# Gate products of the second branch in Strassen's form, paired in PSUM banks, copied by ScalarE and added by GpSimd

## The reference

```python
def merge_branches(gates, o_mla, o_conv, o_diff, w_o_mla, w_o_conv, w_o_diff, w_out):
    g = jax.nn.sigmoid(gates).reshape(*gates.shape[:-1], N_BRANCH, D_MODEL)
    y = (g[..., 0, :] * (o_mla @ w_o_mla) + g[..., 1, :] * (o_conv @ w_o_conv)
         + g[..., 2, :] * (o_diff @ w_o_diff))
    return y @ w_out
```

## Time and profile before

| what | value |
|---|---|
| median of 3 runs | 1467.52 us (1464.31 to 1472.09) |
| the profiled execution: its time | 1470.08 us |
| its span, first to last instruction | 1468.3 us |
| PE busy | 1386.8 us, 94% of the span |
| DVE busy | 799.1 us, 54% |
| ACT busy | 368.1 us, 25% |
| POOL busy | 209.9 us, 14% |
| mean granted TensorE clock | 0.986 of full speed |
| chain of waits that ended last | PE 84%, DMA 6%, DVE 4%, SP's queue 3%, ACT 2% |

### The profile page before, as it was taken

How to read it: one execution, slowest core, us unless ns; L and a number is a source line. 1 busy time by engine, 2 the same in 40 slices (tenths; PEclk the granted TensorE clock), 3 DMA queues, 4 the chain that set the end, 5 groups by cost and what they waited for, 6 DMA issues and landing times.

```text
span 1468.3 us, 19532 instructions
## 1 busy us (share of the span) xinstructions
PE 1386.8 (94%) x7590; PEld 819.1 (56%) x7590; DVE 799.1 (54%) x1758; ACT 368.1 (25%) x803; POOL 209.9 (14%) x146
## 2 busy tenths in 40 slices
PE   5999999999999999989997979999999999999886
PEld 3444447754444445655554537744668885666553
DVE  2679954778887953533131118894763443434333
ACT  4112414532223012222221224141542202100001
POOL 0220524200011210012221210152000110000000
PEclk9999999999999999999999998999999999999899
DMA  9412220144535447299999968232533478999996
GB/s 379 166 36 89 83 77 38 59 158 161 183 100 201 161 192 320 102 343 419 417 419 420 415 264 347 94 115 77 202 123 144 162 303 361 401 420 420 420 420 260
DMA packets 59551, 347.66 MB, mean 237 GB/s; under 512 B 8388, under 2 KB 15172, under 8 KB 28352
## 3 DMA queue, kind: packets, MB, share of 16 engines
q1 hardware_dynamic: 53856, 335.86, 57.8%
q0 software_dynamic: 5024, 8.40, 1.5%
q10 hardware_dynamic: 576, 2.10, 0.4%
HBM read 343.44 MB, written 11.80 MB: 242 GB/s over the span
## 4 chain that ended last, share of the span: by engine, by line
PE 84%; DMA 6%; DVE 4%; SPq 3%; ACT 2%; issue 1%; DVEq 0%; POOLq 0%; ACTq 0%
PE bank L467 79%; DMA arena<-w_up_in 5%; ACT arena L1335 2%; PE bank L834 2%; SPq L3061 2%; PE bank L567 1%; DVE arena L1818 1%; PE bank L1209 1%; DMA x<-x_in 1%; DMA arena<-y 0%; PE bank L1229 0%; DVE am L2104 0%; SPq L3109 0%; SPq L3095 0%; DVE arena L2209 0%
## 5 line engine op out<-in xcount | busy, mean ns | idle before, releaser
L467 PE MATMUL bank<-arena 128*128 128x512 f32 (+10 forms) x5912 | 1194.6, 437 | 23.3 <-DMA arena<-w_up_in 12.9
L467 PEld LDWEIGHTS bank<-arena 128*128 128x128 f32 (+4 forms) x5912 | 655.6, 161 | 484.1 <-issue 360.4
L1335 ACT ACTIVATE arena<-bank 128x512 f32<-128x512 f32 (+5 forms) x423 | 200.7, 494 | 904.6 <-PE bank L467 805.0
L1818 DVE SCALAR_TENSOR_TENSOR arena<-arena,bank 64x256 f32<-64x256 f32 (+2 forms) x121 | 57.9, 479 | 247.7 <-ACT arena L1335 182.3
L1818 DVE SCALAR_TENSOR_TENSOR arena<-arena,early 128x512 f32<-128x512 f32 (+1 forms) x254 | 177.6, 773 | 0.4
L2104 DVE TENSOR_REDUCE am<-bank 128x1 f32<-128x512 f32 (+1 forms) x96 | 55.5, 599 | 107.8 <-PE bank L467 107.6
L2879 POOL TENSOR_TENSOR arena<-arena 128x512 f32<-128x512 f32 (+1 forms) x32 | 37.3, 1166 | 368.4 <-DVE arena L1818 368.4
L1335 ACT ACTIVATE arena<-bank,am 128x512 f32<-128x512 f32 (+1 forms) x96 | 58.6, 613 | 80.8 <-DVE am L2107 80.6
L2918 POOL DMA_INDIRECT y<-arena,routing x33 | 32.9, 998 | 181.2 <-ACT arena L1335 181.2
L834 PEld LDWEIGHTS bank<-con,arena 128*128 128x128 f32 x240 | 29.9, 141 | 26.1 <-issue 11.9
L834 PE MATMUL bank<-con,arena 128*128 128x128 f32 x240 | 38.6, 275 | 5.1 <-DVE arena L2119 4.6
(11 more groups left out here) (242 smaller groups left out, 929.4 us busy)
## 6 DMA issues: line engine op xcount, KB each, us to landing
arena<-w_gate_in SPq DMA_DIRECT2D x60, 1024.0 KB, 22.0
arena<-w_up_in SPq DMA_DIRECT2D x60, 1024.0 KB, 24.5
arena<-w_down_in SPq DMA_DIRECT2D x45, 1024.0 KB, 22.8
arena<-mg_in SPq DMA_DIRECT2D x12, 2048.0 KB, 8.0
arena<-adaT_in SPq DMA_DIRECT2D x40, 512.0 KB, 3.6
arena<-adaT_in SPq DMA_DIRECT2D x16, 1024.0 KB, 7.1
arena<-ada_in SPq DMA_DIRECT2D x6, 2048.0 KB, 15.5
arena<-mo_in SPq DMA_DIRECT2D x6, 2048.0 KB, 7.8
```

Source lines behind the costliest of these rows:

```text
L467: return nc.tensor.matmul(out, w, rhs, start=start, stop=stop)
L1335: return nc.scalar.activation(out, in_, fn, **kw)
L1818: return V.scalar_tensor_tensor(out, in0, sc, in1, op0=op0, op1=op1)
```

## The change

The gates of b = 1 in layer 0 become grouped too, in a form of their own: `GROUPED` is ((0, 1), ()), and branch 1 has 112 steps in place of 64. PE's seven products of a group go in four PSUM tiles of class "a", two products to a bank (128x256 each; the seventh alone). ACT copies each tile to one of two temporaries in SBUF (`pair_tmp`), and all the adding is POOL's: after pair 1 "v" (512 columns, two outputs) and "u" (256), after pair 2 "12" and "w" (256 each), after pair 3 "lower" (512), beside the four weight sums of a group. Then one tanh over both tiles. ACT waits for POOL ahead of copies whose temporary POOL still reads. DVE adds nothing for b = 1. Signs in the first branch change so that both branches share `h_sums`; there operations change from add to subtract or back, and one scalar_tensor_tensor becomes a tensor_tensor. POOL's order for a group is `sums_behind`, `pair_upper`, `sums_ahead` of the next group, `pair_lower`.

```diff
--- before.py
+++ after.py
@@ -181,6 +181,7 @@
...
+        pair_tmp = [qa[:, 5, :], qa[:, 7, :]]
...
         PRODUCTS = 7
-        GROUPED = ((0,), ())
+        GROUPED = ((0, 1), ())
         N_GROUPS = 4 * len(GROUPED[0])
...
@@ -274,14 +275,19 @@
         def gate_steps(l, b):
             return 16 * PRODUCTS if b in GROUPED[l] else KD * KD
 
+        STEPS = [("tokens", 0, 0)]
+        STEPS += [("s1", 0, 0), ("s2", 0, 0)]
+        for n_ in range(N_GROUPS):
+            key_ = divmod(n_, 4)
+            STEPS += [(w_, *key_) for w_ in (("s4", "s3", "u") if key_[0] == 0 else ("s4", "s3", "v", "u"))]
+            if n_ < N_GROUPS - 1:
+                STEPS += [(w_, *divmod(n_ + 1, 4)) for w_ in ("s1", "s2")]
+            STEPS += [(w_, *key_) for w_ in (("corner",) if key_[0] == 0 else ("12", "w", "lower"))]
+        step_at = {w_: n_ + 1 for n_, w_ in enumerate(STEPS)}
+
         def pool_sums(what, b, g):
 
-            n = 4 * b + g
-            if what == "corner":
-                return 6 * n + (9 if n < N_GROUPS - 1 else 7)
-            if n == 0 and what in ("s1", "s2"):
-                return {"s1": 2, "s2": 3}[what]
-            return 6 * n + {"s1": 1, "s2": 2, "s4": 4, "s3": 5, "u": 6}[what]
+            return step_at[what, b, g]
...
@@ -310,7 +316,12 @@
                 if b in GROUPED[l]:
                     if r < gates_ and r % 4 == 3:
                         done.append(("product", b, divmod(r // 4, PRODUCTS)))
-                    if r >= 4 * PRODUCTS and (r - 3) % (4 * PRODUCTS) == 0 and r < gates_ + 4:
+                    if b == 1:
+                        if r >= 4 * PRODUCTS and (r - 7) % (4 * PRODUCTS) == 0 and r < gates_ + 8:
+                            done.append(("gates", b, (r - 7) // (4 * PRODUCTS) - 1))
+                        if r < gates_:
+                            continue
+                    elif r >= 4 * PRODUCTS and (r - 3) % (4 * PRODUCTS) == 0 and r < gates_ + 4:
                         done.append(("gates", b, (r - 3) // (4 * PRODUCTS) - 1))
                 elif r < gates_ and r % KD == KD - 1:
                     done.append(("gate", b, r // KD))
...
+                def paired_step(b, g, i):
+
+                    p, k = divmod(i, 4)
+                    key = (f"mg{2 * b + g // 2}", l, 0)
+                    if g % 2 == 0 and i == 0:
+                        unit(key)
+                    w = ring[:, unit_no[key] % NRING, :].rearrange("p (c k m) -> p c k m", c=4, k=KD)
+                    c = 2 * g % 4
+                    w11, w12, w21, w22 = w[:, c, 0:4], w[:, c, 4:8], w[:, c + 1, 0:4], w[:, c + 1, 4:8]
+                    first, second = slice(0, CTX), slice(CTX, T)
+                    tile, lhs, rhs, needs = ((0, w11, h[:, 0:4, first], None), (0, w21, h_sums[0], "s1"),
+                                             (1, w12, h[:, 4:8, first], None), (1, weight_sum, h_sums[1], "s2"),
+                                             (2, w11, h[:, 4:8, second], "s4"), (2, w21, h_sums[2], "s3"), (3, w22, h_sums[3], None))[p]
+                    if i % 8 == 0:
+                        begin("a", ("pair", l, b, g, tile))
+                    if k == 0 and needs:
+                        pe.wait_ge(sums_ready, pool_sums(needs, b, g))
+                    at = 256 * (p % 2)
+                    ins = mm(bank_of[("pair", l, b, g, tile)][:, at:at + 256], lhs[:, k, :], rhs[:, k, :], k == 0, k == 3)
+                    if i % 8 == 7 or i == 4 * PRODUCTS - 1:
+                        end("a", ins)
+                        if g % 2 == 1 and p == PRODUCTS - 1:
+                            used(key, "a")
+
...
                             branch_step(b, (r - gate_steps(l, b)) // 4, r % 4)
                         elif b in GROUPED[l]:
-                            group_step(b, r // (4 * PRODUCTS), r % (4 * PRODUCTS))
+                            (paired_step if b else group_step)(b, r // (4 * PRODUCTS), r % (4 * PRODUCTS))
                         else:
...
@@ -1581,6 +1616,20 @@
                 def group_tile(b, g, p):
 
                     t1, t2 = gate_tiles(b, g)
+                    if b == 1:
+                        if p % 2 or p == PRODUCTS - 1:
+                            ps = take(("pair", l, b, g, p // 2))
+                            if p == 1 and g:
+                                act.wait_ge(sums_ready, pool_sums("lower", b, g - 1))
+                            elif p == 5:
+                                act.wait_ge(sums_ready, pool_sums("v", b, g))
+                            elif p == 3 and g:
+                                act.wait_ge(sums_ready, pool_sums("w", b, g - 1))
+                            cols = slice(0, 256 if p == PRODUCTS - 1 else 512)
+                            if p == PRODUCTS - 1:
+                                act.wait_ge(sums_ready, pool_sums("v", b, g))
+                            give(f(pair_tmp[p in (3, 5)][:, cols], ps[:, cols], ACT.Copy))
+                        return
                     if p in (0, 1):
...
@@ -1590,6 +1639,11 @@
                 def gates_tanh(b, g):
 
                     t1, t2 = gate_tiles(b, g)
+                    if b == 1:
+                        both_ = gt8[:, 2 * g:2 * g + 2, :]
+                        act.wait_ge(sums_ready, pool_sums("lower", b, g))
+                        f(both_, both_, ACT.Tanh, scale=0.5).then_inc(gates_done, 1)
+                        return
                     act.wait_ge(empty["d"], Dn[("z", l, b, g)])
...
                             branch(b, c)
-                        elif what == "product":
+                        elif what == "product" and b == 0:
                             group_tile(b, *c)
...
@@ -2827,31 +2881,58 @@
                     G.tensor_tensor(w21, w21, w22, op=ADD).then_inc(sums_ready, 1)
                     pool.wait_ge(sums_ready, pool_sums("s1", b, g))
                     if (b, g) != (0, 0):
-                        pool.wait_ge(full["d"], Dn[("r", l) + ((b, g - 1) if g else (b - 1, 3))])
+                        if b == 1 and g:
+                            pool.wait_ge(full["a"], A[("pair", l, b, g - 1, 1)])
+                        else:
+                            pool.wait_ge(full["d"], Dn[("r", l) + ((b, g - 1) if g else (b - 1, 3))])
                     G.tensor_tensor(weight_sum, w11, w21, op=ADD).then_inc(sums_ready, 1)
...
 
                     _, w11, w12, w21, w22 = group_weights(b, g)
-                    pool.wait_ge(full["a"], A[("q", l, b, g)])
+                    pool.wait_ge(full["a"], A[("pair", l, b, g, 0) if b else ("q", l, b, g)])
                     G.tensor_tensor(w11, w12, weight_sum, op=ADD).then_inc(sums_ready, 1)
-                    pool.wait_ge(full["a"], A[("x", l, b, g)])
+                    if b == 0:
+                        pool.wait_ge(full["a"], A[("x", l, b, g)])
                     G.tensor_tensor(w21, weight_sum, w22, op=SUB).then_inc(sums_ready, 1)
                     pool.wait_ge(sums_ready, pool_sums("s3", b, g))
+
+                def pair_upper(b, g):
+
+                    tiles = gt8[:, 2 * g:2 * g + 2, :]
+                    t1, t2 = tiles[:, 0], tiles[:, 1]
+                    pool.wait_ge(empty["a"], A[("pair", l, b, g, 1)])
+                    G.tensor_tensor(tiles[:, :, 0:256], pair_tmp[0][:, 0:256].unsqueeze(1).to_broadcast([128, 2, 256]),
+                                    grid(pair_tmp[1], 2), op=ADD).then_inc(sums_ready, 1)
+                    pool.wait_ge(sums_ready, pool_sums("v", b, g))
+                    G.tensor_tensor(t1[:, 256:512], t2[:, 0:256], pair_tmp[0][:, 256:512], op=SUB).then_inc(sums_ready, 1)
+                    pool.wait_ge(sums_ready, pool_sums("u", b, g))
+
+                def pair_lower(b, g):
+
+                    tiles = gt8[:, 2 * g:2 * g + 2, :]
+                    t1, t2 = tiles[:, 0], tiles[:, 1]
+                    pool.wait_ge(empty["a"], A[("pair", l, b, g, 2)])
+                    G.tensor_tensor(t1[:, 256:512], t1[:, 256:512], pair_tmp[1][:, 0:256], op=ADD).then_inc(sums_ready, 1)
+                    G.tensor_tensor(t2[:, 256:512], pair_tmp[1][:, 256:512], t2[:, 0:256], op=SUB).then_inc(sums_ready, 1)
+                    pool.wait_ge(sums_ready, pool_sums("w", b, g))
+                    pool.wait_ge(empty["a"], A[("pair", l, b, g, 3)])
+                    G.tensor_tensor(grid(t2[:, :], 2), t2[:, 256:512].unsqueeze(1).to_broadcast([128, 2, 256]),
+                                    grid(pair_tmp[0], 2), op=ADD).then_inc(sums_ready, 1)
...
@@ -2868,10 +2949,10 @@
                 if l == 0:
                     for n in range(1, N_GROUPS):
                         sums_behind(n // 4, n % 4)
-                        upper(n // 4, n % 4)
+                        (pair_upper if n >= 4 else upper)(n // 4, n % 4)
                         if n < N_GROUPS - 1:
                             sums_ahead((n + 1) // 4, (n + 1) % 4)
-                        corner(n // 4, n % 4)
```

(12 more changed lines are left out.)

8 lines of the change are left out of this document (2 added, 6 removed).

## The result

The changed kernel takes **1478.88 us** (median of 6 runs, 1476.92 to 1485.94) against 1468.76 for the kernel before beside it (6 runs, 1464.31 to 1472.09): a ratio of **1.0065**, 95% interval 1.0041 to 1.0089. It is slower, by 10.1 us. The profiled execution is the slowest of the six, 1485.94 us, with a span of 1484.1. Lines have moved: the product helper is L478, the transposition L869, ACT's helper L1370, DVE's `stt` L1872, the column products L2260 and L2263, the maxima L2158, `out_d` L2187; POOL's sums s1, s2, s4, s3 are L2881, L2888, L2895, L2898, and v, u, 12, w, lower are L2906, L2909, L2917, L2918, L2921.

What follows compares the result with a forecast made beforehand. PE was taken as the bound, DVE second and the bound afterwards: +10.4 - 1.0 + 2.3 + 1.5 = +13.2 us on 1470.08 gave 1483.3, or 1481 us against the median; range 1472 to 1494.

Steps and rivals of the forecast that it cites:

- PE, -6.7: Second branch's gate products, layer 0: 112 half-width products replace 64, saving PE 6.7 us only while PE stays the bound.
- Holding, 6.5 us a group: Second branch's gate stage: POOL's 9.4 us of sums per group hold DVE's SBUF instructions for 6.5 us.
- Stage +10.4: Seven units, 354.21 to 416.23: DVE becomes the bound at 20.7 us per two units, 72.5 against 62.0 us.
- Start -1.0: First unit of the stage: DVE has room and PE is ahead by part of a unit's saving, -1.0 us.
- Tail into units 40 and 41, +2.3: Units 40 and 41: the last group's remaining POOL sums run in where DVE is already the bound, +2.3 us.
- PE late on s1, +1.5: Second product of a group: PE waits for a POOL weight sum, 0.5 us late in three groups, +1.5 us.
- Behind unit 47: shifts with PE: What lies behind unit 47 is triggered by PE's progress and shifts with it.
- POOL's sums in DVE's idle time: Rival, units 33 to 39: sums fall into DVE's idle time and beside PSUM reads, PE stays bound; not slower, chance 0.12.
- ScalarE's bank wait: Rival: each group's last product waits for a bank behind ScalarE's exponentials, 1.9 us a group, 7.6 in all; chance 0.07.
- The clock: Rival: PE's waits behind DVE lower its clock once a group, 6.8 us on top of the forecast, 1488; chance 0.13.
- ScalarE's extra 2 us a group: ScalarE's added copies and wider tanh, replacing two tanhs: about 2 us more a group, off the path.
- the 3.00 us hole of the earlier trace: A DVE column product waits 3.00 us for a column behind mg4's load; closes with DVE late, +3 should it stay.

Runs made afterwards that it cites:

- E4: Changed kernel without the second column product per unit in units 32 to 39, the five left over moved behind unit 47: 1484.02 us, ratio 1.0102.
- E5: Kernel before with the second column product per unit dropped in units 32 to 39, the five left over moved behind unit 47: 1492.37 us, ratio 1.0168.
- E3: Changed kernel with POOL's 34 sums cut to 16 columns each, order and waits kept: 1465.35 us, ratio 0.9971.
- E1: Kernel before plus 34 unused sums on POOL beside the second branch's gates: 1481.3 us, ratio 1.0083.
- E2: Kernel before plus 40 memsets of 128x1024 on POOL beside the second branch's gates: 1469.58 us, ratio 1.0004.
- E8: Kernel before plus 34 unused sums made by DVE itself behind the second column of units 32 to 39: 1482.99 us, ratio 1.0097.

## Why the prediction was right

It was right in sign and mechanism: DVE became the bound because POOL's sums hold its column products. Step by step:

- **PE, -6.7, not cashed.** E4 shows the gain where DVE does not stand in the way: units 33 to 39 4.45 us shorter than E5's, the two units ahead of them 13.78 against 14.50, together 5.2 us at the least, as PE still waited for `out_d` there. E3 shows the whole time fall by 0.3%. In the changed kernel itself only the start is cashed.
- **Holding, 6.5 us a group.** Measured 6.1 in the round above, 65% of POOL's own 9.4 us against the 69% forecast. The price of a full collision, taken from the earlier trace rows at 2.28 - 1.22 = 1.06, came back three times as 1.06 to 1.07, where a 128x512 sum ran into a column product. The discount was not for PSUM reads alone: 12 and w met scalings of probabilities in SBUF and cost only 0.41 and 0.35 of their 0.73.
- **Stage +10.4.** Measured 72.19 - 62.02 = +10.2; E1 gives +10.7 with sums alone. That it came so close is partly luck, as the two windows of units 33 to 39 show, before and after:

```profile
354.21:416.23 62.02, 62.02 (x203) 30.12 (x202) 53.60 (x117) 15.37 (x42) 0.00 (x0) 1.00 0.47 161
351.90:424.09 72.19, 62.07 (x288) 49.65 (x287) 71.44 (x114) 21.44 (x52) 45.92 (x29) 0.93 0.38 131
```

  The forecast took 3.5 x 14.2 = 49.7 us for DVE's own work there, and it was 53.6: the mean of 7.1 a unit took in unit 32, which has only 3.3 us of it, while the earlier trace rows had shown 7.6. It took 3.5 x 6.5 = 22.8 us of holding, and DVE's busy time grew by 17.8: these units hold 29 of the 34 sums, and the last column product slipped behind them. One term was 3.9 us too small, the other 4.9 too large.
- **Start -1.0.** Measured 13.78 - 14.50 = -0.7 for units 31 and 32.
- **Tail into units 40 and 41, +2.3.** Units 40 to 46 took 40.19 instead of 38.69: +1.5, somewhat less.
- **PE late on s1, +1.5.** This term failed: PE waits nowhere for a sum of POOL's. I had added a delay of PE to a forecast in which PE was no longer the bound; what PE loses beside the bound is not paid again.
- **Behind unit 47: shifts with PE.** 100.72 us both before and after; nothing was made up and nothing lost.

The sum is +11.0 instead of +13.2, nearly all of the difference the term of s1 and the tail, and the medians differ by 10.1. The forecast of 1481 is only 2 us over the median because the kernel before, too, took 1.2 us more in this comparison (1468.76) than the 1467.52 that the forecast set out from.

The rivals: **POOL's sums in DVE's idle time** would have needed at most 3.6 us of holding a group; it was 6.1. DVE's idle time did pay 7.8 of 18.9 us, as the ledger shows. **ScalarE's bank wait** appeared once, in the first group, 1.61 us against the 1.9 worked out, and not again, since DVE was later than ScalarE from then on. **The clock** did fall: behind three long waits the granted clock was 0.72, 0.66 and 0.72 over 6, 5 and 6 us, a mixture of the two levels, so (1 - 0.72) x 6 = 1.7 us of PE each, the figure assumed. What failed was to price it on top of the forecast: it counts only where PE is the bound afterwards, and PE was not. The changed signs, ScalarE's extra 2 us a group and the new wait on SP cost nothing that the trace shows; the 3.00 us hole of the earlier trace rows closed, as forecast.

No version here beats the kernel before. E3, the only faster one, leaves work out. What the change could bring if the sums cost DVE nothing is not settled by it: it gains 3.5 us in all with the larger hole of mg4's load in it, and E4 against E5 gains 5.2 us in the attention with the sums in full. Making the second branch's sums for two of its four groups only, so that the holding fits into DVE's idle time, was not tried.

## What to carry to other kernels

Before work goes from TensorE to GpSimd, look in that stage for the engine that is second, not at GpSimd's idle time: in eight units with 10 us of slack on VectorE, sums that hold it for 19 us turn a saving of 5 us into a loss of 10. A sum on GpSimd beside two-input VectorE work in SBUF costs VectorE about as much as making the sum itself (in the round above 0.27 to 1.07 us for 128x512, 0.84 in the mean, against 0.69; 0.31 to 0.41 for 128x256 against 0.43; and 72.68 against 71.87 us for the stage), so "GpSimd is free there" has to be shown by a collision in the trace, not by its busy time. Work moved out of a full stage takes its buffers and the loads behind them along: follow those before calling the new place empty.

## What was not expected of the hardware

Neither point stood in the prediction; the expectations of E2 and E8 reckoned with them before those runs showed them.

That GpSimd's memsets hold some of VectorE's instructions and not others: beside the same 953 ns memsets a tensor_scalar of two columns went from 170 to 782 ns, while two-input products of 128x1024 stayed at 1216. The Trainium skill, SBUF — State Buffer, section "Who interferes with whom", draws this line: instructions with two SBUF inputs contend with GpSimd instructions that read SBUF, not with those that only write it, while tensor_scalar can run in two-port modes, and there it contends with GpSimd, without that exception. The trace agrees with the first half (1216 ns beside the memsets). The 782 ns fit the second, but no run here shows in which mode those tensor_scalars ran.

That a cost for VectorE is nearly the same whether GpSimd or VectorE itself does the adding. E1 and E8 differ by 0.8 us in 72, although nothing in the two mechanisms makes them equal: in one DVE waits, in the other it works.
